# RWKV pair of a two-layer hybrid block: the eight raw ticks and the closing steps regrouped into four ticks

## What is computed

```python
def _wkv_scan(r, w, k, v, kk, a, s0, reverse):
    def step(S, inp):
        r_t, w_t, k_t, v_t, kk_t, a_t = inp
        sa = jnp.einsum('bhvk,bhk->bhv', S, kk_t)
        S = (S * w_t[:, :, None, :] - sa[..., None] * (kk_t * a_t)[:, :, None, :]
             + v_t[..., None] * k_t[:, :, None, :])
        return S, jnp.einsum('bhvk,bhk->bhv', S, r_t)
```

## Time and profile before

| | before |
|---|---|
| median of 3 runs | 2586.5 us |
| the profiled execution | 2591.72 us |
| its span | 2589.9 us |
| granted TensorE clock, mean | 0.984 |
| instructions | 46521 |
| DVE busy | 805.2 us (31%) |
| ACT busy | 574.8 us (22%) |
| POOL busy | 233.7 us (9%) |

### The profile page before, as it was taken

One profiled execution on the slowest core, in us unless ns is written; L12 is line 12 of the kernel. 1 busy time (PEld: TensorE's weight loads), 2 busy tenths in 40 slices (PEclk: granted clock), 3 DMA queues, 4 the chain that ended last, 5 costly groups with the idle time before them and its releaser, 6 DMA issues. The chain is left out here.

```text
span 2589.9 us, 46521 instructions
## 1 busy us (share of the span) xinstructions
PE 2490.4 (96%) x20808; PEld 1476.5 (57%) x20808; DVE 805.2 (31%) x1651; ACT 574.8 (22%) x1233; POOL 233.7 (9%) x243
## 2 busy tenths in 40 slices
PE   6999999999999999999999999999999999999998
PEld 4444654455555554444444445556466667687887
DVE  2542333253444432121010002441555554321101
ACT  3353323122223211020000002441332323111100
POOL 0000000122222300000000000010022323000000
PEclk9999999999999999999999999999999899899999
DMA  7102111233232334222222224112122111145443
GB/s 285 50 17 73 42 57 49 90 105 110 67 139 68 132 111 151 73 98 81 74 75 79 73 81 151 49 66 90 41 83 67 51 59 60 61 138 177 154 155 106
DMA packets 64391, 238.81 MB, mean 92 GB/s; under 512 B 7009, under 2 KB 8049, under 8 KB 63425
## 3 DMA queue, kind: packets, MB, share of 16 engines
q1 hardware_dynamic: 61824, 220.23, 25.1%
q0 software_dynamic: 2368, 15.61, 1.6%
HBM read 234.76 MB, written 1.05 MB: 91 GB/s over the span
## 5 line engine op out<-in xcount | busy, mean ns | idle before, releaser
L420 PE MATMUL psum<-normed,panel_ring 128*128 128x512 f32 (+1 forms) x3136 | 1166.4, 517 | 5.1 <-ACT normed L648 4.1
L420 PEld LDWEIGHTS psum<-normed,panel_ring 128*128 128x128 f32 x3136 | 575.6, 191 | 425.6 <-issue 374.0
L420 PE MATMUL psum<-arena,panel_ring 128*128 128x512 f32 (+1 forms) x1792 | 609.8, 494 | 1.8 <-ACT arena L1067 1.8
L420 PE MATMUL psum<-arena 64*64 64x64 f32 (+5 forms) x12696 | 522.0, 251 | 41.6 <-ACT arena L739 10.3
L420 PEld LDWEIGHTS psum<-arena 64*64 64x64 f32 (+2 forms) x12696 | 343.3, 141 | 334.1 <-issue 214.6
L420 PEld LDWEIGHTS psum<-arena,panel_ring 128*128 128x128 f32 x1792 | 335.2, 191 | 225.7 <-issue 200.3
L714 DVE TENSOR_REDUCE softmax_stats<-psum 128x1 f32<-128x512 f32 (+1 forms) x144 | 83.8, 600 | 178.8 <-PE psum L420 177.7
L739 ACT ACTIVATE arena<-psum,softmax_stats 128x512 f32<-128x512 f32 (+1 forms) x144 | 87.7, 613 | 220.0 <-PE psum L697 111.0
L1819 DVE TENSOR_TENSOR arena<-arena 128x512 f32<-128x512 f32 (+1 forms) x64 | 35.8, 559 | 305.8 <-ACT arena L1806 305.8
L1695 DVE SCALAR_TENSOR_TENSOR arena<-psum,modulation,arena 128x256 f32<-128x256 f32 x24 | 10.9, 480 | 313.9 <-PE psum L420 313.9
L1571 POOL TENSOR_SCALAR arena<-arena 128x64 f32<-128x64 f32 x96 | 72.2, 766 | 323.2 <-DVE arena L1617 178.1
(11 more groups left out here) (159 smaller groups left out, 1379.2 us busy)
## 6 DMA issues: line engine op xcount, KB each, us to landing
panel_ring<-panels SPq DMA_DIRECT2D x398, 512.0 KB, 3.3
arena<-panels SPq DMA_DIRECT2D x16, 512.0 KB, 14.8
arena<-small_b POOLq DMA_DIRECT2D x2, 2176.0 KB, 9.9
arena<-bias_d POOLq DMA_DIRECT2D x2, 2048.0 KB, 9.2
arena<-x_t SPq DMA_DIRECT2D x2, 1024.0 KB, 7.4
arena<-x_t POOLq DMA_DIRECT2D x1, 2048.0 KB, 14.4
arena<-const_r POOLq DMA_DIRECT2D x2, 800.0 KB, 6.6
arena<-small_c POOLq DMA_DIRECT2D x2, 768.0 KB, 4.7
```

Of the source, the lines that this page charges most:

```text
L420: return nc.tensor.matmul(out, lhsT, rhs, start=start, stop=stop, skip_group_check=check)
```

## The change

`RAW` goes from 8 to 4. On TensorE a tick holds two raw products where it held one: the transposed values and the first product of be and ar; the second, and the product of ar and be; both products of ka and ar; both transposes. The yields of ACT, POOL and DVE are regrouped to match: the core's DVE program no longer begins with an empty step, and POOL masks both halves of m13 in one step. `CORE_FILL` has 38 entries and not 42, so the same fills are spread over fewer ticks. The close of the pair before is placed two steps a tick in the first four ticks, and not one a tick in the first eight. No instruction is added or taken away.

```diff
--- before.py
+++ after.py
@@ -227,7 +227,7 @@
     return g, t, r
 
 
-PREP, RAW, LEVEL_STEPS, SCAN, CLOSE = 17, 8, 2 * (LEVELS - 1), 3 * NCH, 8
+PREP, RAW, LEVEL_STEPS, SCAN, CLOSE = 17, 4, 2 * (LEVELS - 1), 3 * NCH, 8
 CORE_FILL = [2] * RAW + [2] * LEVEL_STEPS + [2] * SCAN
 
 
@@ -1394,7 +1394,6 @@
 
             e.wait_ge(mixed.h, n_z)
             to_tokens((0, 1), lambda d: v).then_inc(s_v.h, 1)
-            yield
             e.wait_ge(s_op.h, s_op.at(3))
             for n in range(2):
                 if n == 1:
@@ -1405,7 +1404,8 @@
                         p = mm(psum[tside(d, hd), 2 - 2 * n + d, j * P:(j + 1) * P], be[half[hd], d, token(c)],
                                ar[half[hd], d, c, :, :].rearrange("p a b -> p (a b)"), True, True)
                 p.then_inc(raw_full.h, 1)
-                yield
+                if n == 0:
+                    yield
             e.wait_ge(raw_dve.h, raw_dve.at(1))
             for c in range(NCH):
                 for d, hd in units:
@@ -1525,15 +1524,14 @@
                 p = nc.scalar.activation(vt[:, d], chunked(psum[:, d, :]), ACT.Copy)
             p.then_inc(s_vc.h, 1)
             yield
-            yield
-            yield
             for n, (dst, bank) in enumerate(((nt, 2), (m13[:, :, 0:4], 0), (m13[:, :, 4:8], 2), (bt, 0), (kt, 2))):
                 e.wait_ge(raw_full.h, raw_full.at(n + 3))
                 for d in range(2):
                     out = dst[:, d].rearrange("p c a b -> p (c a b)") if n in (1, 2) else dst[:, d].rearrange("p c t -> p (c t)")
                     p = nc.scalar.activation(out, psum[:, bank + d, :], ACT.Copy)
                 p.then_inc(raw_act.h, 1)
-                yield
+                if n % 2 == 0:
+                    yield
             for j in range(1, LEVELS):
                 bb = 2 if j % 2 else 0
                 e.wait_ge(b_full.h, b_full.at(j))
@@ -1552,15 +1550,15 @@
             for d in range(2):
                 p = nc.gpsimd.tensor_copy(X[:, d], eye.unsqueeze(1).broadcast_to([P, NCH, CHUNK]))
             p.then_inc(s_eye.h, 1)
-            yield from idle(5)
+            yield from idle(3)
             for n in range(2):
                 e.wait_ge(raw_act.h, raw_act.at(n + 2))
                 for d in range(2):
                     piece = m13[:, d, 4 * n:4 * n + 4].rearrange("p c a b -> p c (a b)")
                     p = nc.gpsimd.tensor_tensor(piece, piece, consts[:, d * R_DIR:d * R_DIR + P].unsqueeze(1).broadcast_to([P, 4, P]), ALU.mult)
                 p.then_inc(masked.h, 1)
-                yield
-            yield from idle(RAW - 7 + LEVEL_STEPS)
+            yield
+            yield from idle(RAW - 4 + LEVEL_STEPS)
             link(e, nc.gpsimd.tensor_scalar(bonus, kssum, col("r_k", ft), None, ALU.mult))
             nc.gpsimd.tensor_tensor(bonus, r, bonus, ALU.mult).then_inc(s_bon.h, 1)
             yield from idle(3)
@@ -1584,7 +1581,7 @@
                     p = nc.vector.copy_predicated(X[:, d, h4], wide(level(d, 0), 4), pair[:, :, 0, :])
                 p.then_inc((raw_dve if n == 0 else x_ready).h, 1)
                 yield
-            yield from idle(RAW - 3)
+            yield from idle(RAW - 2)
             for j in range(1, LEVELS):
                 tb = 0 if j % 2 else 2
                 e.wait_ge(x_ready.h, x_ready.at(j))
@@ -2019,8 +2016,8 @@
                 others.insert(1 if others[0][1] < 8 else 0, whole(projected[p + 1]))
             for tick, n in enumerate(spread(share, CORE_FILL)):
                 place(core, 1)
-                if p and tick < CLOSE:
-                    place(pairs[p - 1][2], 1)
+                if p and tick < CLOSE // 2:
+                    place(pairs[p - 1][2], 2)
                 if p < PAIRS - 1 and tick > RAW + LEVEL_STEPS:
                     while projected[p + 1].placed < projected[p + 1].steps:
                         fill(others, 1)
```

## The result

The changed kernel took 2601.1 us (median of 4 runs, 2598.3 to 2605.1) where the kernel before, with one more run, took 2586.5 us. The ratio is 1.0059, 95% interval 1.0041 to 1.0078: slower, by 15 us where 28 us were forecast. A later set of runs, both kernels on one chip, gave 2603.3 against 2584.5 us, ratio 1.0071 (1.0049 to 1.0094), so the loss is better put at 15 to 19 us.

A forecast was written before the change was run, and what follows sets the result against it. TensorE, busy 96% of the span, was taken as the bound; -6.4 + 23.3 + 1.1 + 10 = +28 us on 2586.5 gave 2614.5 us, forecast 2608 to 2628, range 2599 to 2634 us.

The forecast's parts named there:

- Part 2: Close of the pair before: waits for DVE's add (+12.8 us) and ACT's square (+10.5 us) lose their cover.
- (d): Close's inputs come earlier, DVE not held by the masks; y_sum costs nothing, half the waits stay; 2597 us, chance 0.06.
- Part 1: Raw ticks: 32 fewer fill bursts between small products, 0.20 us each, -6.4 us.
- Part 3: Fills shifted among ticks: waits for mixing in level ticks +2.5 us, with other waits +1.1 us, kept -5 to +7.
- Part 4: TensorE's clock in the pairs: new waits bring falls to 1.2 GHz, +10 us, from -22 to +30.
- (a): Waits only: close waits cost their 23.3 us, clock falls as many as before; 2604 us, chance 0.25.
- (b): Clock frees itself in layer 1's level ticks, no new wait brings a fall; 2582.5 us, chance 0.06.
- (c): Long clock falls behind four or five close waits of layer 1, 6.8 us each; 2630 to 2640 us, chance 0.15.
- signs named: In the pairs: TensorE's idle time grows by about 23 us, clock in the windows below 0.99 and 0.95.

The follow-up runs named there:

- e1: The changed kernel with the close one step a tick in eight ticks again, raw products still two to a tick; 2565.8 us, ratio 0.9936.
- e3: The kernel before, eight raw ticks of one product, with only the close changed to two steps a tick; 2612.5 us, ratio 1.0125.
- e10: The changed kernel with the empty first DVE step put back and both masks in the second step; 2596.6 us, ratio 1.0057.
- e7: The kernel of e1 with twice the fill in the four raw ticks; 2565.0 us, ratio 0.9925.
- e6: The changed kernel itself once more, beside more runs of the kernel before; 2603.3 us, ratio 1.0071.
- e8: The kernel of e1 with fill weights 2, 3, 2 for raw, level and scan ticks; 2548.3 us, ratio 0.9856.

## Why the prediction was right, and where a size was off

**Part 2, the close's two waits, held within a tenth.** Forecast were 2.26 and 1.99 us for the add in layers 0 and 1, and 1.85 and 1.64 for the square. Measured were 2.20 in layer 0 for the add and 1.72 for the square (above), 1.94 and 1.51 to 1.57 in layer 1, and in all 12.4 us for the add in pairs 1 to 3 and 9.8 us for the square, where 12.8 and 10.5 stood. e1 took both away, so they are shown to be caused by the squeezed close; e3 made the first anew without the joins, and one for the bonus product in place of the second. e10 shows what holds the add: the masks for 4.5 us, as the prediction had it, and close behind them ACT's copies, which it did not name. So rival (d) would not have made the wait free even if it had been right on the masks. No later close wait appeared in the changed kernel, as forecast.

**Part 1, the joins, was under-priced.** "32 x 0.20 = -6.4 us", with 7 as the far end, is the term that was mis-sized. e7 gives 15 us. I had priced only the fill's side, and that side held: in e7 a fill of eight instructions takes 3.63 us, 0.21 less than two of four. The products' side (0.15 us a join) was not in a row of before, and I bounded it from below only, by a smaller gain, where a further gain was as possible.

**Part 3, the fills, was off by 2.6 us.** The level ticks' waits went from 12.7 to 14.9 us, +2.2, where +2.5 was laid out for the mixings and -0.5 for pair 0 of layer 0 (its 1.55 us became 0.99, about 1.0 forecast). The modulation turns lost 3.7 us of waits, not 0.9. That makes -1.5 us and not +1.1, within the -5 to +7 kept for it. In pair 1 of layer 0 the 1.96 and 2.27 us became one of 1.10 us (0.5 forecast). Pair 2 of layer 0 has two of 1.10, as forecast. Layer 1 got the bad ones: 1.96, 2.81 and 2.08 in pair 1 (1.5, 2.2 and 1.9 forecast), 1.10 and 2.38 in pair 2 (1.1 and 1.9 forecast). The last of them, on PE's timeline:

```profile
2145.05 1.94 PE L420 MATMUL psum<-arena 64*64 64x32 f32 x64 [2.38 <-DVE arena L1592]
```

**Part 4, the clock, was right in its sum, and in part by luck.** Forecast were +10 us, and e6 has +9. The forecast was 32 us of low clock in the pairs less the 22 us of before. In the profiled execution of the changed kernel the low clock costs about 26 us there, counted over windows, only 4 us more than the 22. The 9 us come out between the medians because the profiled execution of before had a lower clock (0.984) than the runs of that kernel have on average (0.987), so that 22 us was more than its usual cost. The parts were off as well. Of the twelve close waits five, and not eight, were followed by a low clock, each time for about 1.7 us lost. In pair 1 of layer 0 waits of 2.20 and 1.72 us brought nothing, in pair 2 the same two brought a short stretch each (windows as above, the clock third from the end):

```profile
646.00:660.00 14.00, 10.91 (x205) 7.30 (x207) 3.82 (x10) 4.63 (x9) 0.03 (x1) 1.00 0.44 151
759.00:780.00 21.00, 17.07 (x206) 9.58 (x202) 6.16 (x14) 7.94 (x13) 1.92 (x2) 0.84 0.09 27
```

The pairs of layer 1 have one long stretch at 1.2 GHz, with the 2.38 us just shown, and not three:

```profile
2145.00:2160.00 15.00, 14.95 (x238) 11.54 (x239) 5.55 (x10) 3.25 (x5) 3.46 (x3) 0.56 0.11 36
```

In the 15 us behind that wait the clock is 0.56. And two stretches that lost 3.4 us each came behind standstills of only 1.03 and 1.12 us (at 901.9 us, clock 0.72 from 900 to 912; at 1935.4 us, 0.66 from 1935 to 1945), where before each fall in the pairs stood behind 1.5 us or more. So the length of the standstill alone does not tell whether the clock falls. The Trainium skill ("TensorE: Matmul & The Clock Gate", section on HAM oscillation) would have had no part for the clock. Measured, it was about half of the loss, with no wait in the pairs longer than 2.81 us.

The sum, then: +22.2 us of close waits less 15 of joins and 1.5 of fills is about +6, where +7 is seen at full clock, and with +9 of clock some +15 us, with 15 to 19 measured. The forecast of 28 us was 13 too high by the first measurement: 8.6 in the joins, 2.6 in the fills, about 1 each in the waits and the clock. Of the rivals, (a) is nearest in time with 2604 us, but for another reason: the clock did cost more than before, and the larger gain of the joins made up for it. (b) and (d) are out. The long stretches of (c) did not follow a close wait in the changed kernel. Of the signs named, TensorE's idle time in the pairs grew by 18.6 us, not 23, and the clock in the two windows is 0.98 and 0.95, below before in the first only.

What stays open is the last 0.1 us a join, and which standstills of 1 to 2.3 us bring the clock down and which do not. One of 1.77 us ahead of pair 0 in layer 1 brought none, before and after.

## What to carry to other kernels

In a schedule written out by hand, a step that waits needs the cover between its maker and itself, so work placed behind it in the same tick does not count. When ticks are merged, follow each wait of the stages that share them back to its maker and list what its queue does first. Here a whole gain of 15 us was turned into a loss by two such waits of 2 us, six times each. When the main engine changes often between two shapes of work, price both sides of the change. And give the fill to the ticks in which another engine has the longest chain: 2, 3, 2 in place of 2, 2, 2 was worth 12 us by itself.

## What the runs showed of the hardware

A run of 64x64 matmuls that follows another at once saves 0.15 us over one that starts behind 128x128 matmuls and is followed by them (1.97 against 1.09 and 1.03 us), beside the 0.20 us at the fill.

The 20 us between runs of one and the same kernel go with the granted clock: 2572.6 us at 0.993 and 2592.3 us at 0.983, a program on one core. In these kernels fewer standstills of 1.5 us and more in the pairs went with a higher mean clock: 16 in the changed kernel (0.983), 6 before (0.987), one in e8 (0.993). In e8 six runs lay within 5 us, in the changed kernel six within 9. That the standstills cause the falls is argued from this and from the order in time, not shown: the same waits of 2.20 and 1.72 us were followed by a low clock in one pair and not in another.
